# Attention outputs computed turned: values as weights, probabilities as moving data

## The chip, the cores and the metric

The kernel runs on one core of a Trainium2 chip, in float32. The metric is the device time of one execution in microseconds, the median of several runs. TensorE multiplies; VectorE (DVE), ScalarE (ACT) and GpSimd (POOL) do the elementwise work; SyncE (SP) and GpSimd issue transfers.

## The reference

A two-layer network over 18 tiles of 128 tokens: 2 tiles of a prompt (256 tokens) and 16 of a sample (2048 tokens). Each layer normalizes and modulates its input, projects it to 4096 columns, runs four token mixers of four heads of 64, multiplies each by a SiLU gate, and projects back. Two of the mixers are softmax attention, and they are all that the change touches:

```
s_loc = q @ k_near * scale + bias           # window of +-128 tokens, or a neighbourhood in the grid
s_ctx = q @ k_ctx  * scale                  # 256 further tokens; prompt tiles have only 256 own tokens
p = softmax(concat([s_loc, s_ctx]))
o = p @ concat([v_near, v_ctx])             # then o * silu(gate)
```

The window attention ("win") has a sink in its softmax and shares keys and values between heads; the neighbourhood attention ("nei") has a bias table. The two other mixers are retention ("ret") and a gated recurrence ("hg").

## The kernel before

Each engine has its own instruction stream, written out in order; they meet only at semaphores. A layer has these stages: "first" (a part of the projections), "win", "nei", "rest" (retention and the recurrence, and the output projection). The engines meet at a barrier (`gate`) after the first three; TensorE only reports there (`leave`) and goes on.

In an attention stage a unit `u` is one pair of heads of one tile: `tau, p = divmod(u, 2)`. The stage is a loop over 37 slots. In slot `s`, TensorE computes the scores of unit `s` and transposes and weighs unit `s-1`; between these steps it fills in eight projection matmuls (`fill`, L1161), which is one piece of 128x512 per slot. TensorE never needs a unit sooner than a slot after its scores.

- `scores(u)` (L1266, L1270) writes PSUM banks 2 to 5, the two heads of the pair in the two row halves of the array.
- VectorE's `maxima(u)` (L2119 to L2144) adds the mask or bias and finds row maxima; ScalarE's `exps(u)` (L1727) makes the probabilities `a.e`, queries on partitions.
- `turn(u, f)` (L1279) transposes the probabilities, 128 keys at a time and up to four such chunks at once, into bank 6 (`TURN_BANK`). ScalarE (fills 0 and 2) or VectorE (fill 1) copies them to `a.pT` (L1712, L2152).
- `weigh(u, f)` (L1297) multiplies with the values, into bank 7 (`OUT_BANK`). The stationary weights are a half (64 queries) of a chunk of `a.pT`, the moving data are 64 columns of values, and the two halves of the queries go to the two column halves of the array.
- VectorE's `finish(tau)` (L2176) multiplies bank 7 by the gates, which hold one over the softmax's sum (L2168), at the head of slot `2*tau+3`; GpSimd stores the tile.
- `prep(slot)` (L1226) transposes queries and keys for coming units, also through bank 6. In "win" this is in even slots; in "nei" from slot 5 on, queries are in even slots and keys in odd ones.

`fills_of(n)` lists the chunks of a unit with `n` chunks per head. A prompt tile has 2 chunks per head, a sample tile 4 or 5 in "win" and 5 or 6 in "nei", so a unit is one, two or three fills of four or two chunks. `count_attention` plans beforehand who used bank 6 last (`use.before`) and which semaphore count tells that it was emptied.

ScalarE's loop in a slot is: copy the finished projection piece, `take_prep`, `take_turned(.., 0)`, `exps`, `take_turned(.., 2)`, and for pieces of group 6 `bounds_ln` (L1668), two logarithms that wait for VectorE; in "nei" this is in slots 33 and 34. VectorE's is: `finish`, `maxima`, `take_turned`, `weigh_gates`, `gates` (the SiLU of a piece, L2017 to L2022, with a reciprocal), `bounds`, and in "win" `rotate_for`.

Of the kernel before, what the change touches and what calls it, by code (L numbers as in the profile page):

```python
# [13 lines left out]
P = 128  # L14
# [6 lines left out]
HD = 64  # L21
# [198 lines left out]
def fills_of(n):  # L220

    chunks = [(hp, c) for hp in range(2) for c in range(n)]
    return [chunks[i:i + 4] for i in range(0, len(chunks), 4)]
# [48 lines left out]
def count_attention(names, near_of, preps_of, k_inc, q_inc):  # L272
    made, previous = {}, None
    n = Counts()
    for l in range(DEPTH):
        for name in names:
# [7 lines left out]
            def use(key, by_act):  # L284
                nonlocal previous
                u = p.use[key] = Use()
                u.before, previous = previous, u
                n.turned += 1
                u.turned, u.by_act = n.turned, by_act
                if by_act:  # L290
                    n.by_act += 1
                    u.taken = n.by_act
                else:
                    n.by_dve += 1
                    u.taken = n.by_dve

            for slot in range(-2, 2 * NT + 1):
                for item in p.preps.get(slot, ()):
# [11 lines left out]
                if p.preps.get(slot):  # L310
                    use(("prep", slot), True)
                if slot >= 1:
# [35 lines left out]
def build(nc, ins, outs):  # L348
# [49 lines left out]
    def attention(s, name, cq, ck, cv, cg, cache_k, cache_v, col, keys):  # L398
# [5 lines left out]
        a.gate_t = sb(s, f"{name}_gate_t", [P, 2, GW])  # L404
        a.out_t = sb(s, f"{name}_out_t", [P, 2, GW])
        a.qT = sb(s, f"{name}_qT", [P, 2, 2, P])
        a.e = sb(s, f"{name}_e", [P, 2, 2, 6 * P])
# [122 lines left out]
    act_step, dve_step = sem("act_step"), sem("dve_step")  # L530
    yr_step = sem("yr_step")
    rstd_ready = sem("rstd_ready")
# [18 lines left out]
    def gate(eng, l, stage):  # L551
# [11 lines left out]
    scored, nm_ready, e_ready, weighed, out_ready = (  # L563
        sem(x) for x in ("scored", "nm_ready", "e_ready", "weighed", "attention_ready"))
    mask_in, sink_ready = sem("mask_in"), sem("sink_ready")
    bias_in = [sem(f"bias_in{k}") for k in range(3)]
    bias_clear, band_in, neg_ready, tables_out = (sem(x) for x in ("bias_clear", "band_in", "neg_ready", "tables_out"))

    for a, name in ((ret, "ret"), (hg, "hg")):
        (a.bk_ready, a.bkv_done, a.bs_ready, a.kf_ready, a.kv_done, a.sf_ready, a.var_ready, a.r_ready, a.out_ready, a.n_step) = (  # L570
            sem(f"{name}_{x}") for x in ("bk_ready", "bkv_done", "bs_ready", "kf_ready", "kv_done", "sf_ready", "var_ready",
                                         "r_ready", "out_ready", "n_step"))
        a.s_in, a.s_saved, a.clear, a.tab_in, a.p_done, a.p_ready, a.o_done = (
# [7 lines left out]
        sem(f"hg_{x}") for x in ("gated", "qk_ready", "qx_ready", "tc_ready", "ones_ready", "ks_ready"))  # L581
    dec_dve, dec_act = (sem(x) for x in ("dec_dve", "dec_act"))
    bank_turned, bank_taken = sem("bank_turned"), sem("bank_taken")
    y_taken, y_scaled = sem("y_taken"), sem("y_scaled")


    def taken(eng, use):

        if use is not None:
            eng.wait_ge(taken_act if use.by_act else taken_dve, use.taken)  # L590

# [351 lines left out]
    def _(pool):  # L943
# [11 lines left out]
        pool.wait_ge(tables_out, 16)  # L955
        pool.wait_ge(dec_dve, DEC_DVE)
        pool.dma_start(decays, dec_new[:, :, :]).then_inc(tables_out, 16)
# [171 lines left out]
    def _(pe):  # L1129
        pe.wait_ge(consts_in, 48)  # L1130
        pe.wait_ge(setup, SETUP_COND)
        for l in range(DEPTH):
# [65 lines left out]
            for a in (win, nei):  # L1198
# [83 lines left out]
                def weigh(u, f):  # L1282
                    tau, p = divmod(u, 2)
                    n = plan.near(tau) + CT
                    if f == 0 and p == 0:
                        need(pe, out_ready, plan.tile + tau)
                        if a is nei:
# [5 lines left out]
                    for i, (hp, c) in enumerate(fills_of(n)[f]):  # L1293
                        h = head_of(a, p, hp)
                        for half in range(2):
                            at = i * P + half * HD
                            last = nc.tensor.matmul(ps[half * HD:(half + 1) * HD, OUT_BANK, h * HD:(h + 1) * HD], a.pT[:, f, at:at + HD],  # L1297
                                                    values_of(tau, h)[c], start=(c == 0), stop=(c == n - 1))
                    last.then_inc(weighed, 1)

                fill(LEAD * KC)
# [288 lines left out]
    def _(act):  # L1590
# [5 lines left out]
        act.wait_ge(vectors_in, 16 * (2 * DEPTH + 8))  # L1596
        decay = Own(act, dec_act)
        for d in range(DEPTH):
            at = DEC_DVE // DEPTH * d
            act.wait_ge(dec_dve, at + 2)  # L1600
# [3 lines left out]
            act.wait_ge(dec_dve, at + 6)  # L1604
            decay.mark(nc.scalar.activation(dec_new[:, d, D_PAIR:D_PAIR + 4].rearrange("p (a g) -> p a g", g=2), lgp[:, :, :],
# [8 lines left out]
            for h in range(HEADS):  # L1614
                act.wait_ge(dec_dve, at + 7 + 3 * h)
# [4 lines left out]
        own = Own(act, act_step)  # L1620
        for l in range(DEPTH):
# [59 lines left out]
            for a in (win, nei):  # L1681
# [32 lines left out]
                def exps(u):  # L1714
# [22 lines left out]
                for slot in range(2 * NT + 1):  # L1737
                    piece = pieces[slot - 1 + LEAD] if slot > 0 else None
                    if piece:
                        take_piece(*piece)  # L1740
# [8 lines left out]
                    if piece and piece[0] == 6:  # L1749
                        bounds_ln(*piece)  # L1750
                gate(act, l, a.stage)
            pieces = PROJ_ORDER["rest"]

            def norm_stats(a, t):
                u, st = l * NT + t, a.st[:, t % 2]
                steps = Steps(act, a.n_step, u)
                act.wait_ge(a.var_ready, u + 1)
                steps.mark(nc.scalar.activation(st[:, 2], st[:, 1], ACT.Ln, bias=eps[:, 0:1], scale=1.0 / HD))
                steps.wait()
                nc.scalar.activation(st[:, 3], st[:, 2], ACT.Exp, scale=-0.5).then_inc(a.r_ready, 1)  # L1760
# [79 lines left out]
            def scale_y(t):  # L1840
                u, b = l * NT + t, t % 2
                steps = Steps(act, yr_step, u * 2)
                act.wait_ge(y_taken, 2 * u + 2)
                need(act, yr_ready, u)
                rstd(y_t[:, b], b, steps, yr_ready, y_sq[:, :], y_stat)

# [61 lines left out]
    def _(dve):  # L1908
# [33 lines left out]
        dve.wait_ge(vectors_in, 16 * (2 * DEPTH + 8))  # L1942
        decay = Own(dve, dec_dve)
        for d in range(DEPTH):
            at = DEC_ACT // DEPTH * d
            if d > 0:
                dve.wait_ge(dec_act, at)
# [3 lines left out]
            dve.wait_ge(dec_act, at + 2)  # L1951
            decay.mark(nc.vector.tensor_scalar(lg_t[:, 2], lg[:, d], 0.0, None, ALU.min))
# [6 lines left out]
            dve.wait_ge(dec_act, at + 9)  # L1959
            keys = dec_new[:, d, D_KEY:D_KEY + 2 * HEADS]  # L1960
            decay.mark(nc.vector.tensor_scalar(keys, keys, HD ** -0.5, None, ALU.mult))
            for h in range(HEADS):
                dve.wait_ge(dec_act, at + 9 + 2 * (h + 1))
                decay.mark(nc.vector.tensor_tensor(dtmp[:, 0], dtmp[:, 0], dtab[:, 2], ALU.mult))
# [4 lines left out]
        assert decay.n == DEC_DVE, decay.n  # L1969
        own = Own(dve, dve_step)  # L1970
        for l in range(DEPTH):
# [103 lines left out]
            for a in (win, nei):  # L2075
# [446 lines left out]
```

## Time and profile before

| | |
|---|---|
| runs | 4083.63 us median of 3 (4082.23 to 4086.58) |
| the profiled execution | 4087.09 us, span 4085.3 us, mean granted TensorE clock 0.968 |
| TensorE busy | 3830.6 us (94%), 24448 matmul records |
| VectorE, ScalarE, GpSimd busy | 2406.2 us (59%), 1204.5 us (29%), 572.2 us (14%) |
| chain that ended last | TensorE 85%, VectorE 7%, ScalarE 2%, DMA 2% |

A busy share is an average over stages. Matmuls are pipelined, so a record's duration is longer than the distance between two starts; the timeline's start times say what a group of matmuls takes. A float32 matmul leaves two records, a transpose one.

### The profile page before, as it was taken

The page shows a single profiled execution, that of the slowest core. Times are in us where ns is not written, and L with a number is a line of the kernel's source. Part 1 is how long each engine was busy: PE and PEld are TensorE (multiplying, and loading weights), DVE is VectorE, ACT ScalarE, POOL GpSimd, SP SyncE. Part 2 cuts the span into 40 slices and gives each one's busy share as a digit, 9 for nine tenths or more (in the row PEclk, how much of TensorE's full clock was granted, in tenths as well). Part 3 has the DMA queues.
Part 4 walks back from the last instruction along what each step waited for, and adds up shares of the span by engine and source line. Part 5 has one row for each costly group of instructions (what it writes and reads, how often), then busy time and mean ns, then how long its engine had stood idle before and what let it go on. Part 6 is the DMA issues. An engine that isn't in the chain of part 4 may idle for free.

```text
span 4085.3 us, 63551 instructions
## 1 busy us (share of the span) xinstructions
PE 3830.6 (94%) x24448; PEld 2070.8 (51%) x24448; DVE 2406.2 (59%) x4838; ACT 1204.5 (29%) x3401; POOL 572.2 (14%) x870
## 2 busy tenths in 40 slices
PE   5999999999998998899999999999999989979997
PEld 2544555545554455455544445554555445555554
DVE  3223345323666887899932333552256688879996
ACT  2411232223331122344443022222333212224443
POOL 2000000100000254110000000001000005521000
PEclk7999999999998998899999999999999999979999
DMA  7432121132222334223333021113222233333222
GB/s 233 126 132 96 56 68 53 61 105 67 87 79 92 114 102 153 93 97 113 116 109 97 39 95 50 68 43 120 74 77 73 85 104 118 107 127 122 96 94 69
DMA packets 247772, 388.91 MB, mean 95 GB/s; under 512 B 42736, under 2 KB 163440, under 8 KB 247344
## 3 DMA queue, kind: packets, MB, share of 16 engines
q1 hardware_dynamic: 207504, 262.55, 20.7%
q0 software_dynamic: 39968, 122.30, 8.2%
q8 instruction: 195, 3.19, 0.3%
q14 instruction: 105, 0.86, 0.1%
HBM read 264.42 MB, written 122.25 MB: 95 GB/s over the span
## 4 chain that ended last, share of the span: by engine, by line
PE 85%; DVE 7%; ACT 2%; DMA 2%; SPq 2%; issue 2%; POOLq 1%; POOL 0%; ACTq 0%; DVEq 0%
PE ps L1161 47%; PE ps L1511 12%; PE ps L1297 5%; PE ps L1279 4%; PE ps L1266 3%; PE ps L1464 2%; PE ps L1270 2%; PE ps L1429 1%; DVE ret_qd L2255 1%; PE ps L1408 1%; ACT mT L1810 1%; DVE e_t L2019 1%; PE ps L1339 1%; PE ps L1226 1%; PE ps L1489 1%
## 5 line engine op out<-in xcount | busy, mean ns | idle before, releaser
L1161 PE MATMUL ps<-w_sb,hT 128*128 128x512 f32 x4608 | 2204.2, 612 | 3.7 <-ACT hT L1642 2.4
L1161 PEld LDWEIGHTS ps<-w_sb,hT 128*128 128x128 f32 x4608 | 815.8, 192 | 768.8 <-issue 729.9
L1511 PE MATMUL ps<-wo_sb,mT 128*128 128x512 f32 x1152 | 533.1, 607 | 50.8 <-ACT mT L1810 50.8
L979 POOL DMA_DIRECT2D projected<-row_t x252 | 138.2, 548 | 2483.1 <-DVE row_t L2022 1086.1
L2019 DVE RECIPROCAL e_t<-e_t 128x256 f32<-128x256 f32 (+1 forms) x180 | 430.8, 2393 | 6.2
L1511 PEld LDWEIGHTS ps<-wo_sb,mT 128*128 128x128 f32 x1152 | 209.3, 191 | 282.7 <-issue 212.2
L2017 DVE TENSOR_SCALAR e_t<-e_t 128x256 f32<-128x256 f32 (+1 forms) x180 | 71.1, 395 | 238.9 <-ACT row_t L1660 207.8
L1654 ACT ACTIVATE row_t<-ps 128x512 f32<-128x512 f32 x108 | 64.5, 597 | 394.3 <-PE ps L1161 351.8
L2119 DVE TENSOR_REDUCE nei_st<-ps 128x2 f32<-128x512 f32 x72 | 49.8, 691 | 208.7 <-PE ps L1270 208.7
L2152 DVE COPY win_pT<-ps 128x512 f32<-128x512 f32 x64 | 44.3, 692 | 213.4 <-PE ps L1279 213.4
L2152 DVE COPY nei_pT<-ps 128x512 f32<-128x512 f32 x64 | 44.3, 692 | 207.8 <-PE ps L1279 207.8
L2119 DVE TENSOR_REDUCE win_st<-ps 128x2 f32<-128x512 f32 x72 | 49.6, 690 | 193.8 <-PE ps L1270 193.8
L2316 DVE TENSOR_TENSOR hg_q<-hg_d,hg_xT 128x256 f32<-128x256 f32 x252 | 153.0, 607 | 12.5 <-issue 6.1
L1712 ACT ACTIVATE win_pT<-ps 128x512 f32<-128x512 f32 (+1 forms) x128 | 64.5, 504 | 313.3 <-PE ps L1279 313.3
L1279 PEld LDWEIGHTS ps<-ident,nei_e 128*128 128x128 f32 x736 | 92.8, 141 | 105.6 <-issue 103.0
L1712 ACT ACTIVATE nei_pT<-ps 128x512 f32<-128x512 f32 (+1 forms) x136 | 74.4, 547 | 242.9 <-PE ps L1279 242.9
L1659 ACT ACTIVATE e_t<-ps 128x256 f32<-128x256 f32 x108 | 41.3, 382 | 350.7 <-PE ps L1161 349.9
L2351 DVE TENSOR_REDUCE hg_tc<-hg_w 128x64 f32<-128x448 f32 x144 | 132.9, 923 | 4.9
L1279 PEld LDWEIGHTS ps<-ident,win_e 128*128 128x128 f32 x656 | 83.6, 141 | 102.2 <-issue 100.3
L1999 DVE TENSOR_SCALAR xt<-xt,stat 128x1024 f32<-128x1024 f32 x36 | 27.1, 755 | 174.2 <-ACT stat L1630 174.2
L1297 PEld LDWEIGHTS ps<-win_v,win_pT 128*64 128x64 f32 x2624 | 92.0, 137 | 73.8 <-issue 73.2
L1829 ACT ACTIVATE hg_p<-hg_tc 64x64 f32<-64x64 f32 x288 | 73.2, 254 | 177.5 <-DVE hg_tc L2351 174.9
(243 smaller groups left out, 5355.1 us busy)
## 6 DMA issues: line engine op xcount, KB each, us to landing
projected<-row_t POOLq DMA_DIRECT2D x288, 256.0 KB, 2.8
w_sb<-in_w_in SPq DMA_DIRECT2D x14, 2048.0 KB, 9.3
wa<-in_w_ada SPq DMA_DIRECT2D x16, 1536.0 KB, 8.0
hg_raw<-projected SPq DMA_DIRECT2D x72, 256.0 KB, 4.8
out_streams<-y_t POOLq DMA_DIRECT2D x36, 512.0 KB, 4.2
hg_braw<-projected SPq DMA_DIRECT2D x108, 128.0 KB, 2.4
hg_raw<-projected SPq DMA_DIRECT2D x36, 384.0 KB, 5.2
mx_t<-mixed SPq DMA_DIRECT2D x36, 384.0 KB, 4.6
```

Source lines behind the costliest of these rows:

```text
L979: pool.dma_start(rows[tok(t), g * GRP:(g + 1) * GRP], row_t[:, p.slot]).then_inc(row_stored[p.slot], 16)
L1161: mm = nc.tensor.matmul(ps[:, p.bank, :], hT[:, k, t * P:(t + 1) * P], w_sb[:, g % 2, k, :], start=(k == 0), stop=(k == KC - 1))
L1266: nc.tensor.matmul(s[:, 0:n], q, k, start=True, stop=True)
L1279: last = nc.tensor.transpose(ps[:, TURN_BANK, i * P:(i + 1) * P], a.e[:, u % 2, hp, c * P:(c + 1) * P], ident[:, :])
L1297: last = nc.tensor.matmul(ps[half * HD:(half + 1) * HD, OUT_BANK, h * HD:(h + 1) * HD], a.pT[:, f, at:at + HD], values_of(tau, h)[c], star ...
L1511: mm = nc.tensor.matmul(ps[:, 6 + g, :], mT[:, t % 2, k, :], wo_sb[:, k, g * GRP:(g + 1) * GRP], start=(k == 0), stop=(k == KC - 1))
L1712: nc.scalar.activation(a.pT[:, f, 0:n], ps[:, TURN_BANK, 0:n], ACT.Copy).then_inc(taken_act, 1)
L2019: own.mark(nc.vector.reciprocal(e, e))
L2119: own.mark(nc.vector.reduce_max(st[:, MX, pair_at], both[:, :, n:n + CTX], AX_X))
L2152: nc.vector.tensor_copy(a.pT[:, 1, 0:n], ps[:, TURN_BANK, 0:n]).then_inc(taken_dve, 1)
L2316: own.mark(nc.vector.tensor_tensor(halves(q), halves(d, size + s, TO_END * size), halves(x), ALU.mult))
L2351: nc.vector.tensor_reduce(hg.tc[:, h % 2, :], hg.w[:, :, :].rearrange("p s n -> p n s"), AX_X, ALU.add).then_inc(hg.tc_ready, 1)
```

## The change

`weigh` takes the values as weights (128 keys by 64) and a whole chunk of `a.pT` (128 keys by 128 queries) as moving data. One matmul replaces two. Each head's output then stands turned (64 features on partitions, 128 queries in columns), the two heads of the pair in the two column halves of the array; `fills_of` is reordered so that the heads alternate. Outputs of a tile fill `OUT_BANK` as before. ScalarE copies them to `a.oT` (`take_out`) at the head of its slot `2*tau+3`, before it copies the projection piece. TensorE transposes the two 128x128 blocks into bank 6 (`turn_out`), after the scores of that slot, or at the end of the loop for the last tile. `finish` then waits for `turn_out` and reads bank 6 instead of bank 7; for "win" with the heads' order rearranged. The next user of bank 6 waits for `finish`. `weigh` waits for ScalarE's copy (`out_taken`) where it waited for `finish`. Besides, several own-order semaphores are merged into one per engine.

```diff
-    chunks = [(hp, c) for hp in range(2) for c in range(n)]
+    chunks = [(hp, c) for c in range(n) for hp in range(2)]
...
-            for slot in range(-2, 2 * NT + 1):
+            for slot in range(-2, 2 * NT + 2):
+                if slot >= 3 and slot % 2 == 1:
+                    use(("o", (slot - 3) // 2), None)
...
+        a.oT = sb(s, f"{name}_oT", [P, 2, P])
...
-            eng.wait_ge(taken_act if use.by_act else taken_dve, use.taken)
+            eng.wait_ge(out_ready if use.by_act is None else taken_act if use.by_act else taken_dve, use.taken)
...
                     if f == 0 and p == 0:
-                        need(pe, out_ready, plan.tile + tau)
+                        need(pe, out_taken, plan.tile + tau)
...
-                        for half in range(2):
-                            at = i * P + half * HD
-                            last = nc.tensor.matmul(ps[half * HD:(half + 1) * HD, OUT_BANK, h * HD:(h + 1) * HD], a.pT[:, f, at:at + HD],
-                                                    values_of(tau, h)[c], start=(c == 0), stop=(c == n - 1))
+                        last = nc.tensor.matmul(ps[hp * HD:(hp + 1) * HD, OUT_BANK, p * P:(p + 1) * P], values_of(tau, h)[c],
+                                                a.pT[:, f, i * P:(i + 1) * P], start=(c == 0), stop=(c == n - 1))
                     last.then_inc(weighed, 1)
+
+                def turn_out(tau):
+
+                    use = plan.use["o", tau]
+                    pe.wait_ge(out_taken, plan.tile + tau + 1)
+                    taken(pe, use.before)
+                    for p in range(2):
+                        last = nc.tensor.transpose(ps[:, TURN_BANK, p * P:(p + 1) * P], a.oT[:, p, :], ident[:, :])
+                    last.then_inc(turned_in, 1)
...
                         scores(slot)
+                        if slot >= 3 and slot % 2 == 1:
+                            turn_out((slot - 3) // 2)
                         fill(1)
...
+                turn_out(NT - 1)
                 leave(pe)
...
+                def take_out(tau):
+                    act.wait_ge(weighed, plan.weighed[2 * tau + 1, len(fills_of(plan.near(tau) + CT)) - 1])
+                    if tau > 0:
+                        act.wait_ge(turned_in, plan.use["o", tau - 1].turned)
+                    nc.scalar.activation(a.oT[:, :, :], ps[:, OUT_BANK, 0:GW].rearrange("p (k n) -> p k n", n=P), ACT.Copy
+                                         ).then_inc(out_taken, 1)
...
+                    if slot >= 3 and slot % 2 == 1:
+                        take_out((slot - 3) // 2)
                     if piece:
                         take_piece(*piece)
...
-                    dve.wait_ge(weighed, plan.weighed[2 * tau + 1, len(fills_of(plan.near(tau) + CT)) - 1])
+                    dve.wait_ge(turned_in, plan.use["o", tau].turned)
...
-                    nc.vector.tensor_tensor(a.out_t[:, b], ps[:, OUT_BANK, 0:GW], a.gate_t[:, b], ALU.mult).then_inc(out_ready, 1)
+                    out, o, g = a.out_t[:, b], ps[:, TURN_BANK, 0:GW], a.gate_t[:, b]
+                    if a is win:
+                        out, g = (x.rearrange("t (k p n) -> t p k n", k=2, n=HD) for x in (out, g))
+                        o = o.rearrange("t (p k n) -> t p k n", k=2, n=HD)
+                    nc.vector.tensor_tensor(out, o, g, ALU.mult).then_inc(out_ready, 1)
```

## Rows read from the trace of the kernel before

**Rows 1.** The page's part 4: the chain that ended last, by line.
```profile
PE ps L1161 47%; PE ps L1511 12%; PE ps L1297 5%; PE ps L1279 4%; PE ps L1266 3%; PE ps L1464 2%; PE ps L1270 2%; PE ps L1429 1%; DVE ret_qd L2255 1%; PE ps L1408 1%; ACT mT L1810 1%; DVE e_t L2019 1%; PE ps L1339 1%; PE ps L1226 1%; PE ps L1489 1%
```

**Rows 2.** Windows in "win" and "nei", layer 0: width, busy (instructions) by engine, clock, DMA.
```profile
400.00:790.00 390.00, 390.00 (x2569) 214.24 (x2568) 180.90 (x482) 113.58 (x299) 31.03 (x55) 1.00 0.17 54
850.00:1239.00 389.00, 389.00 (x2661) 213.78 (x2660) 201.13 (x344) 123.58 (x270) 28.20 (x50) 1.00 0.24 75
```

**Rows 3.** Groups by line and form, TensorE: the transposes of probabilities.
```profile
L1279 PE MATMUL ps<-ident,nei_e 128*128 128x128 f32 x736 | 113.8, 274 | 1.7 <-ACT nei_pT L1712 1.4 <-DVE nei_pT L2152 0.3
L1279 PE MATMUL ps<-ident,win_e 128*128 128x128 f32 x656 | 103.1, 273 | 1.5 <-ACT win_pT L1712 1.5
```

**Rows 4.** Timeline of TensorE in "nei" into an odd slot: start, us, line, records.
```profile
1004.09 0.69 PE L1297 MATMUL ps<-nei_v,nei_pT 128*64 128x64 f32 x16
1004.71 1.13 PE L1161 MATMUL ps<-w_sb,hT 128*128 128x512 f32 x2
...
1009.35 1.13 PE L1266 MATMUL ps<-nei_kT,nei_qT 64*128 64x512 f32 x4
1010.31 0.60 PE L1270 MATMUL ps<-nei_kT_past,nei_qT 64*128 64x256 f32 x4
1010.84 1.12 PE L1161 MATMUL ps<-w_sb,hT 128*128 128x512 f32 x2
1011.80 0.60 PE L1226 MATMUL ps<-ident,nei_k_raw 128*128 128x128 f32 x4
1012.24 1.88 PE L1161 MATMUL ps<-w_sb,hT 128*128 128x512 f32 x4
```

**Rows 5.** Timeline of TensorE in "win": a fill of two chunks, and the next group.
```profile
639.17 0.45 PE L1297 MATMUL ps<-win_v,win_pT 128*64 128x64 f32 x8
639.55 0.92 PE L1266 MATMUL ps<-win_kT,win_qT 64*128 64x384 f32 x4
```

**Rows 6.** Timelines of TensorE in other stages: groups with 128 moving columns.
```profile
304.27 1.92 PE L1139 MATMUL ps<-wa,cond 128*2 128x128 f32 x48
306.13 2.41 PE L1161 MATMUL ps<-w_sb,hT 128*128 128x512 f32 x5
...
1411.87 0.71 PE L1387 MATMUL ps<-ret_xT 64*128 64x128 f32 x8
1412.51 1.98 PE L1161 MATMUL ps<-w_sb,hT 128*128 128x512 f32 x4
```

**Rows 7.** Timeline of VectorE in the same odd slot.
```profile
1010.95 0.69 DVE L2119 TENSOR_REDUCE nei_st<-ps 128x2 f32<-128x512 f32 x1 [0.74 <-PE ps L1270]
...
1013.20 0.17 DVE L2138 TENSOR_SCALAR nei_st<-nei_st 128x2 f32<-128x2 f32 x1
```

**Rows 8.** Timeline of ScalarE in the same odd slot.
```profile
1015.09 0.90 ACT L1727 ACTIVATE nei_e<-ps,nei_st 128x768 f32<-128x768 f32 x1
```

**Rows 9.** Timelines of TensorE and ScalarE at the head of "nei" slot 35.
```profile
1229.24 1.98 PE L1161 MATMUL ps<-w_sb,hT 128*128 128x512 f32 x4
...
1230.67 0.36 ACT L1659 ACTIVATE e_t<-ps 128x256 f32<-128x256 f32 x1
```

**Rows 10.** Timelines of TensorE and VectorE at the ends of "win" and "nei".
```profile
793.01 0.69 PE L1297 MATMUL ps<-win_v,win_pT 128*64 128x64 f32 x16 [0.17 <-DVE win_pT L2152]
793.81 0.69 PE L1161 MATMUL ps<-w_sb,hT 128*128 128x512 f32 x1
...
1243.11 0.45 PE L1297 MATMUL ps<-nei_v_past,nei_pT 128*64 128x64 f32 x8
...
1245.05 0.42 DVE L2176 TENSOR_TENSOR nei_out_t<-ps,nei_gate_t 128x256 f32<-128x256 f32 x1
...
1262.94 0.38 PE L1339 MATMUL ps<-ret_braw,ret_bkd 128*64 128x64 f32 x2 [5.13 <-DVE ret_bkd L2222]
```

**Rows 11.** A wait of TensorE in "rest", and a window (clock third from last) after it.
```profile
1464.46 0.66 PE L1408 MATMUL ps<-ret_raw,ret_p 128*128 128x64 f32 x4 [1.19 <-DVE ret_p L2263]
...
1466.10:1469.60 3.50, 3.50 (x8) 1.78 (x6) 2.53 (x1) 0.00 (x0) 0.00 (x0) 0.51 0.10 37
```

More of the change, by code:

```diff
@@ L289, in use @@
                 u.turned, u.by_act = n.turned, by_act
-                if by_act:
+                if by_act is None:
+                    u.taken = p.tile + key[1] + 1
+                elif by_act:
                     n.by_act += 1
@@ L311, in count_attention @@
                     use(("prep", slot), True)
-                if slot >= 1:
+                if 1 <= slot <= 2 * NT:
                     tau = (slot - 1) // 2
@@ L530, in build @@
     act_step, dve_step = sem("act_step"), sem("dve_step")
-    yr_step = sem("yr_step")
     rstd_ready = sem("rstd_ready")
@@ L564, in build @@
         sem(x) for x in ("scored", "nm_ready", "e_ready", "weighed", "attention_ready"))
+    out_taken = sem("out_taken")
     mask_in, sink_ready = sem("mask_in"), sem("sink_ready")
@@ L569, in build @@
     for a, name in ((ret, "ret"), (hg, "hg")):
-        (a.bk_ready, a.bkv_done, a.bs_ready, a.kf_ready, a.kv_done, a.sf_ready, a.var_ready, a.r_ready, a.out_ready, a.n_step) = (
+        (a.bk_ready, a.bkv_done, a.bs_ready, a.kf_ready, a.kv_done, a.sf_ready, a.var_ready, a.r_ready, a.out_ready) = (
             sem(f"{name}_{x}") for x in ("bk_ready", "bkv_done", "bs_ready", "kf_ready", "kv_done", "sf_ready", "var_ready",
-                                         "r_ready", "out_ready", "n_step"))
+                                         "r_ready", "out_ready"))
         a.s_in, a.s_saved, a.clear, a.tab_in, a.p_done, a.p_ready, a.o_done = (
@@ L581, in build @@
         sem(f"hg_{x}") for x in ("gated", "qk_ready", "qx_ready", "tc_ready", "ones_ready", "ks_ready"))
-    dec_dve, dec_act = (sem(x) for x in ("dec_dve", "dec_act"))
     bank_turned, bank_taken = sem("bank_turned"), sem("bank_taken")
-    y_taken, y_scaled = sem("y_taken"), sem("y_scaled")
+    y_taken = sem("y_taken")
     def taken(eng, use):
         if use is not None:
-            eng.wait_ge(taken_act if use.by_act else taken_dve, use.taken)
+            eng.wait_ge(out_ready if use.by_act is None else taken_act if use.by_act else taken_dve, use.taken)
     def piece_out(eng, p):
@@ L955, in _ @@
         pool.wait_ge(tables_out, 16)
-        pool.wait_ge(dec_dve, DEC_DVE)
+        pool.wait_ge(dve_step, DEC_DVE)
         pool.dma_start(decays, dec_new[:, :, :]).then_inc(tables_out, 16)
@@ L1596, in _ @@
         act.wait_ge(vectors_in, 16 * (2 * DEPTH + 8))
-        decay = Own(act, dec_act)
+        own = decay = Own(act, act_step)
         for d in range(DEPTH):
             at = DEC_DVE // DEPTH * d
-            act.wait_ge(dec_dve, at + 2)
+            act.wait_ge(dve_step, at + 2)
             decay.mark(nc.scalar.activation(lg_t[:, 1], lg_t[:, 1], ACT.Exp))
@@ L1603, in _ @@
             decay.mark(nc.scalar.activation(lg_t[:, 1], lg_t[:, 1], ACT.Ln, bias=ones[:, 0:1]))
-            act.wait_ge(dec_dve, at + 6)
+            act.wait_ge(dve_step, at + 6)
             decay.mark(nc.scalar.activation(dec_new[:, d, D_PAIR:D_PAIR + 4].rearrange("p (a g) -> p a g", g=2), lgp[:, :, :],
@@ L1614, in _ @@
             for h in range(HEADS):
-                act.wait_ge(dec_dve, at + 7 + 3 * h)
+                act.wait_ge(dve_step, at + 7 + 3 * h)
                 for way in range(2):
@@ L1619, in _ @@
         assert decay.n == DEC_ACT
-        own = Own(act, act_step)
         for l in range(DEPTH):
@@ L1750, in _ @@
                         bounds_ln(*piece)
+                take_out(NT - 1)
                 gate(act, l, a.stage)
@@ L1755, in norm_stats @@
                 u, st = l * NT + t, a.st[:, t % 2]
-                steps = Steps(act, a.n_step, u)
                 act.wait_ge(a.var_ready, u + 1)
-                steps.mark(nc.scalar.activation(st[:, 2], st[:, 1], ACT.Ln, bias=eps[:, 0:1], scale=1.0 / HD))
-                steps.wait()
+                own.mark(nc.scalar.activation(st[:, 2], st[:, 1], ACT.Ln, bias=eps[:, 0:1], scale=1.0 / HD))
+                own.wait()
                 nc.scalar.activation(st[:, 3], st[:, 2], ACT.Exp, scale=-0.5).then_inc(a.r_ready, 1)
@@ L1841, in scale_y @@
                 u, b = l * NT + t, t % 2
-                steps = Steps(act, yr_step, u * 2)
                 act.wait_ge(y_taken, 2 * u + 2)
                 need(act, yr_ready, u)
-                rstd(y_t[:, b], b, steps, yr_ready, y_sq[:, :], y_stat)
+                rstd(y_t[:, b], b, own, yr_ready, y_sq[:, :], y_stat)
             for m in range(BACK_SLOTS):
@@ L1942, in _ @@
         dve.wait_ge(vectors_in, 16 * (2 * DEPTH + 8))
-        decay = Own(dve, dec_dve)
+        own = decay = Own(dve, dve_step)
         for d in range(DEPTH):
@@ L1946, in _ @@
             if d > 0:
-                dve.wait_ge(dec_act, at)
+                dve.wait_ge(act_step, at)
             decay.mark(nc.vector.tensor_scalar(lg_t[:, 0], lg[:, d], -1.0, None, ALU.mult))
@@ L1950, in _ @@
             decay.mark(nc.vector.tensor_tensor(lg_t[:, 1], lg_t[:, 0], lg[:, d], ALU.min))
-            dve.wait_ge(dec_act, at + 2)
+            dve.wait_ge(act_step, at + 2)
             decay.mark(nc.vector.tensor_scalar(lg_t[:, 2], lg[:, d], 0.0, None, ALU.min))
@@ L1958, in _ @@
                 decay.mark(nc.vector.tensor_copy(lgp[part, :, :], lg[part, d].rearrange("p (a g h) -> p a g h", a=2, g=2)[:, :, :, hp]))
-            dve.wait_ge(dec_act, at + 9)
+            dve.wait_ge(act_step, at + 9)
             keys = dec_new[:, d, D_KEY:D_KEY + 2 * HEADS]
@@ L1962, in _ @@
             for h in range(HEADS):
-                dve.wait_ge(dec_act, at + 9 + 2 * (h + 1))
+                dve.wait_ge(act_step, at + 9 + 2 * (h + 1))
                 decay.mark(nc.vector.tensor_tensor(dtmp[:, 0], dtmp[:, 0], dtab[:, 2], ALU.mult))
@@ L1969, in _ @@
         assert decay.n == DEC_DVE, decay.n
-        own = Own(dve, dve_step)
         for l in range(DEPTH):
```

## The prediction

> **What bounds the kernel now.** I read the chain of waits first, to see which engine carries the time. It names TensorE lines in order of share: the projections (L1161) take 47% of the span, the weighing matmuls that the change rewrites (L1297) 5% [rows 1]. Next I asked for busy time in the two attention stages: in each, TensorE is busy for the whole stretch (390.00 of 390.00 us, 389.00 of 389.00) at granted clock 1.00, while VectorE is busy for about half and ScalarE for less than a third [rows 2]. So here a TensorE instruction added or removed counts in full, and work on the others counts only if TensorE comes to wait for it. The rest is reading TensorE's timeline by start times, since pitches and not durations add up.
>
> **The change on TensorE.** The unit is a chunk of 128 keys for one head; each is transposed once before weighing, and a transpose leaves one record, so there are 736 + 656 = 1392 [rows 3]. Every other matmul leaves two. Before, a chunk is two matmuls (four records) of 64 moving columns, its halves in the two column halves of the array. After, it is one matmul (two records) of 128 moving columns, and the two heads of the pair take the two halves, which the new order in `fills_of` alternates. By the code there are 304 fills of four chunks and 88 of two (304 x 4 + 88 x 2 = 1392).
>
> *Weighing.* From a fill's start to the next group's start: 1004.09 to 1004.71 is 0.62 us for 16 records [rows 4], 639.17 to 639.55 is 0.38 for 8 [rows 5]. The difference, 0.24, is four steps of two parallel records, 0.06 each; what is left, 0.62 - 8 x 0.06, is about 0.15 for entering and draining the split array. For 128 moving columns in column strips the row is L1139: three strips at once, 48 records from 304.27 to 306.13, 16 steps in 1.86, so 0.116 a step with the ends and about 0.11 without [rows 6]. The strips do work in parallel although each has its own moving data. After, a fill of four chunks is then 4 x 0.11 + 0.15 = 0.59, and of two 0.37. The streaming is the same; only some overhead goes. With the rounding of the rows I take -0.025 for each of the 304 (-7.6) and -0.01 for each of the 88 (-0.9): **-8.5 us**. The bound from above is L1387: 8 records of 128 columns, from 1411.87 to 1412.51, 0.64 [rows 6], which would make it +0.02 x 304 + 0.03 x 88 = +8.7. I don't take it because its weights are 128 columns wide, and on entering a mode the weight load lies open: 64 columns are loaded here. The bound from below is a step shorter than 0.11, which is the rival below.
>
> The Trainium skill (TensorEngine Tiling, Performance Considerations, Instruction Overhead) says each matmul carries about 60 cycles of overhead and one with a single column takes as long as one with 60. If that were on top of the streaming, the 1392 steps removed would give, by an estimate from that page, 1392 x 25 ns = -35 us at 2.4 GHz, and the whole change would end near 4070. The rows above leave about 6 ns a step for it, so I keep them.
>
> *Turning back.* New: two 128x128 transposes per tile, 72 tiles. Four transposes go from 1011.80 to 1012.24 [rows 4], so two cost 0.22. They stand between the scores and the first projection matmul, where the array goes back to full mode anyway, so no further switch comes. 66 tiles pay: 66 x 0.22 = **+14.5 us**. Of the other six, two are slot 3 of the neighbourhood stage, just before a wait for keys, and four are at the stage ends, below.
>
> *Waits in an ordinary odd slot.* The new chain is last weighing, ScalarE copy, two transposes, VectorE's gate product, and only then the next user of bank 6. The scores take 1009.35 to 1010.84, 1.49 us [rows 4]; the copy needs some 0.04 + 0.38 + 0.04, ready a second early (0.38 is the kind of 128x256 read at 1230.67, 0.36, in [rows 9]; 0.04 is from the end of the scores, 1010.91, to VectorE's start at 1010.95 [rows 4, 7]). So the transposes don't wait. They end about 0.22 + 0.27 after 1010.84; the product (0.42, as at 1245.05 in [rows 10]) then ends near 1011.8, where the first bank-6 user, the key transposes, stood at 1011.80 and moves to 1012.02 [rows 4]. Its weights want loading some 0.1 earlier, so this is close, and I put 0 on it: nearly 0.1 is left. In window slots three projection matmuls stand before the next user. VectorE's row maximum starts 0.77 later than at 1010.95 and its last step ends near 1014.1 in place of 1013.37 [rows 7]; ScalarE's exponentials start at 1015.09 anyway [rows 8]. The next work of VectorE and of ScalarE waits for TensorE later in the slot, so nothing further is late.
>
> *Neighbourhood slot 35.* The copy of tile 16 stands behind `bounds_ln`, which waits for VectorE. In ScalarE's order the first work behind it starts at 1230.67 [rows 9]. So the copy ends near 1231.05 and the transposes, due at 1229.24, start near 1231.1: TensorE stands 1.9 us, once a layer: **+3.8 us**. Nothing takes it back, as the rest of that stage is paced by TensorE.
>
> *Stage ends.* The last tile has no cover. In the window stage the weighing ends at 793.70 and the projections go on at 793.81 [rows 10]. Now between them: 0.04 + 0.38 + 0.05 for the copy, 0.22 for the first transpose with its weight load, 0.27 for the second, and the same 0.11, 1.07 in all, +0.96: **+1.9 us** for two. At the end of the neighbourhood stage about as much is added, but TensorE then waits 5.13 us for VectorE [rows 10], and VectorE starts its last gate product only at 1245.05, when the weighing has ended at 1243.56 [rows 10]: the turned outputs would be there by 1244.6, so VectorE isn't made later; so +0. Slot 3 goes into the keys' wait likewise.
>
> *Clock.* After a wait of 1.19 us at 1464.46 the granted clock of the next 3.5 us is 0.51, the lower level of 1.2 GHz [rows 11]. One such stretch costs half of it, 1.7 us. Four waits of about that size are new; that one in four is followed by it is my choice: **+1.7**.
>
> Renamed semaphores and the reordered `own` counters order the same instructions in the same way: 0.
>
> Sum: -8.5 + 14.5 + 3.8 + 1.9 + 1.7 = **+13.4 us**. The profiled execution took 4087.1 around its span of 4085.3, so it would read 4100.5; it is 3.5 above the median of the runs, and on the median, 4083.6, I forecast **4097.0**.
>
> **Rivals.** (a) *A wait at bank 6.* If the product ends after the key transposes' due time, each of the 28 neighbourhood slots with keys pays some 0.3: +8, 4105. For it: the 0.1 of room. Against: VectorE is free in time in these slots. (b) *The strips serialize* at 128 columns: +0.43 in each full fill, 304 x 0.43 + 88 x 0.21 = +149, 4246. L1139 speaks against it. (c) *Not slower.* The step of 128 columns is cheaper than 0.11, since each record carries a fixed part. All else costs 21.9, so it decides at 0.07 a fill, a step of 0.09; at 0.085 it gives about -44 + 22, 4062. Against: 0.11 in L1139 and in the transposes alike. (d) *No change to measure*: the entry to the split array gets cheaper by some 0.02 and slot 35 and the clock cost little: -14 + 14.5 + 3 + 2, 4089. A measurement of this kernel tells about 0.2% (8.2 us) from nothing.
>
> **How the numbers follow.** My case 0.65, (a) 0.07, (b) 0.04, (c) 0.07, (d) 0.17. Slower: the first three, 0.76. Same 0.17, faster 0.07. Range: down to (d), up to (a) plus part of the L1387 bound: 4088 to 4110; it leaves out (b), (c) and the far part of that bound.
>
> **What would show it.** Right: L1297 at half its records; fills of 0.59 and 0.37; a pair of transposes in 0.22 right after the scores; TensorE still without waits in ordinary slots; one wait of 1.9 us on ScalarE at slot 35 in each layer. Wrong: a 128-column step other than 0.11, a wait for the gate product before the key transposes, or late maxima that reach TensorE.

## The result, and the profile after

The changed kernel takes 4096.27 us, median of 9 runs (4091.24 to 4098.92), against 4085.20 for the kernel before, median of 9 (4080.36 to 4087.06). The ratio is 1.0028, 95% interval 1.0018 to 1.0039: slower by 11 us, between 7 and 16. The forecast was 13.4 slower, and the measured time lies in its range.

The profiled execution took 4091.24 us around a span of 4089.4. That is the fastest run of this kernel, and the one of before was above all of its own, so the spans (4.1 apart) understate the change. I read the traces for terms, and take totals from the medians.

The chain by line, as in [rows 1], and the two windows of [rows 2] for the changed kernel (L1165 are the projections, L1299 the weighing):

```profile
PE ps L1165 46%; PE ps L1525 12%; PE ps L1299 5%; PE ps L1283 4%; PE ps L1270 3%; PE ps L1478 2%; PE ps L1274 2%; PE ps L1443 1%; DVE ret_qd L2279 1%; DVE e_t L2039 1%; PE ps L1422 1%; ACT mT L1832 1%; PE ps L1353 1%; PE ps L1503 1%; PE ps L1230 1%
```
```profile
400.00:790.00 390.00, 389.26 (x1967) 204.92 (x1968) 180.45 (x482) 118.98 (x317) 31.50 (x56) 1.00 0.17 54
850.00:1239.00 389.00, 387.14 (x1985) 203.39 (x1984) 200.50 (x344) 127.96 (x286) 27.64 (x49) 1.00 0.23 74
```

TensorE still carries both stages: all that it lacks in these windows are one wait of 0.74 that the first window now just takes in, and one of 1.86 in the second.

TensorE's timeline into an odd slot of the neighbourhood stage, against [rows 4], and a fill of two chunks in the window stage, against [rows 5]:

```profile
1004.57 0.66 PE L1299 MATMUL ps<-nei_pT,nei_v 128*64 128x128 f32 x8
1005.15 1.98 PE L1165 MATMUL ps<-w_sb,hT 128*128 128x512 f32 x4
...
1008.62 0.60 PE L1274 MATMUL ps<-nei_kT_past,nei_qT 64*128 64x256 f32 x4
1009.14 0.44 PE L1309 MATMUL ps<-ident,nei_oT 128*128 128x128 f32 x2
1009.42 1.02 PE L1165 MATMUL ps<-w_sb,hT 128*128 128x512 f32 x2
1010.28 0.60 PE L1230 MATMUL ps<-ident,nei_k_raw 128*128 128x128 f32 x4
```
```profile
637.12 0.44 PE L1299 MATMUL ps<-win_pT,win_v 128*64 128x128 f32 x4
637.49 0.92 PE L1270 MATMUL ps<-win_kT,win_qT 64*128 64x384 f32 x4
```

A full fill takes 1005.15 - 1004.57 = 0.58 (0.588 in the mean of the trace's start times, where before had 0.615), one of two chunks 0.37 (0.369 against 0.382). The two transposes (L1309) take 1009.14 to 1009.42, 0.27 to the next start. But the two projection records behind them take 0.86, 1009.42 to 1010.28, where they took 0.96 in [rows 4]: the entry to the full array has moved into the transposes. So the pair costs 0.17 net. The key transposes (L1230) follow without a wait. In the window stage the pair costs the same: 0.27 again, and six projection records behind it take 2.58 where they took 2.68.

VectorE and ScalarE in the same odd slot, against [rows 7] and [rows 8], and TensorE's weight load (PEld) for the key transposes:

```profile
1009.62 0.42 DVE L2200 TENSOR_TENSOR nei_out_t<-ps,nei_gate_t 128x256 f32<-128x256 f32 x1 [1.35 <-PE ps L1309]
...
1012.20 0.17 DVE L2158 TENSOR_SCALAR nei_st<-nei_st 128x2 f32<-128x2 f32 x1
```
```profile
1007.77 0.38 ACT L1748 ACTIVATE nei_oT<-ps 128x256 f32<-128x256 f32 x1 [2.50 <-PE ps L1299]
...
1013.57 0.89 ACT L1740 ACTIVATE nei_e<-ps,nei_st 128x768 f32<-128x768 f32 x1
```
```profile
1010.10 0.54 PEld L1230 LDWEIGHTS ps<-ident,nei_k_raw 128*128 128x128 f32 x4 [0.48 <-DVE nei_out_t L2200]
```

The copy is done at 1008.15, a second before the transposes. The gate product ends at 1010.04, 0.24 before the key transposes start. But their weight load did wait for it: it starts at 1010.10, 0.18 before the first of them, where it started 0.43 ahead in the kernel before. So the product is just in time. The maxima end at 1012.37, still 1.2 before the exponentials begin. All the new work of these two engines is covered here.

Not covered are slot 35 and the stage ends. The first three rows below are TensorE and ScalarE in slot 35, against [rows 9]; the others are TensorE at the stage ends, against [rows 10]:

```profile
1229.67 0.44 PE L1309 MATMUL ps<-ident,nei_oT 128*128 128x128 f32 x2 [1.85 <-ACT nei_oT L1748]
...
1228.74 0.61 ACT L1681 ACTIVATE f_t<-f_t 128x512 f32<-128x512 f32 x1
1229.26 0.36 ACT L1748 ACTIVATE nei_oT<-ps 128x256 f32<-128x256 f32 x1
...
792.44 0.44 PE L1309 MATMUL ps<-ident,win_oT 128*128 128x128 f32 x2 [0.48 <-ACT win_oT L1748]
792.98 1.55 PE L1165 MATMUL ps<-w_sb,hT 128*128 128x512 f32 x3
...
1244.57 0.44 PE L1309 MATMUL ps<-ident,nei_oT 128*128 128x128 f32 x2 [0.49 <-ACT nei_oT L1748]
1245.26 13.97 PE L1165 MATMUL ps<-w_sb,hT 128*128 128x512 f32 x32 [0.26 <-issue]
1262.18 0.70 PE L1353 MATMUL ps<-ret_braw,ret_bkd 128*64 128x64 f32 x8 [2.94 <-DVE ret_bkd L2246]
```

In slot 35 the copy stands behind the logarithms (L1681) and TensorE waits 1.85. TensorE's waits over the whole program (total, times, longest) have two new lines, and one that moves by itself:

```profile
PE ps L1353 <- DVE ret_bkd L2246: 40.2, 12, 6.9
...
PE ps L1230 <- DMA nei_k_raw<-projected: 7.6, 4, 3.0
...
PE ps L1309 <- ACT nei_oT L1748: 4.7, 4, 1.9
...
PE ps L1309 <- ACT win_oT L1748: 1.0, 2, 0.5
```

Added up from the trace: 304 fills x -0.027 and 88 x -0.013 give -9.4; 66 pairs in the slots x 0.174, +11.5 (the two of slot 3 stand before the wait for keys); slot 35, 2 x 1.86, +3.7; window ends, 2 x 0.9, +1.8. That is +8, at the low end of the measured interval.

### The profile page after: what moved, and what is told of

The parts are those of the page before. It is cut to its first block, busy times and chain, and to the rows that moved or that the text cites. A ratio compares the mean times of both kernels' runs of the same rounds, so it can differ in the third digit from the quotient of the medians.

```text
span 4089.4 us, 58483 instructions
## 1 busy us (share of the span) xinstructions
PE 3827.7 (94%) x21808; PEld 2030.7 (50%) x21808; DVE 2403.0 (59%) x4838; ACT 1224.0 (30%) x3473; POOL 572.8 (14%) x870
## 4 chain that ended last, share of the span: by engine, by line
PE 84%; DVE 7%; ACT 3%; SPq 2%; DMA 2%; issue 2%; POOLq 1%; POOL 0%; DVEq 0%; ACTq 0%
PE ps L1165 46%; PE ps L1525 12%; PE ps L1299 5%; PE ps L1283 4%; PE ps L1270 3%; PE ps L1478 2%; PE ps L1274 2%; PE ps L1443 1%; DVE ret_qd L2279 1%; DVE e_t L2039 1%; PE ps L1422 1%; ACT mT L1832 1%; PE ps L1353 1%; PE ps L1503 1%; PE ps L1230 1%
## 5 line engine op out<-in xcount | busy, mean ns | idle before, releaser
L1165 PE MATMUL ps<-w_sb,hT 128*128 128x512 f32 x4608 | 2192.2, 609 | 3.7 <-ACT hT L1655 2.4
L1165 PEld LDWEIGHTS ps<-w_sb,hT 128*128 128x128 f32 x4608 | 814.7, 191 | 782.1 <-issue 766.9
L1098 POOL DMA_DIRECT2D out_streams<-y_t x36 | 21.0, 584 | 719.5 <-DVE y_t L2403 719.5
```

Of the source, the lines that this page charges most:

```text
L1165: mm = nc.tensor.matmul(ps[:, p.bank, :], hT[:, k, t * P:(t + 1) * P], w_sb[:, g % 2, k, :], start=(k == 0), stop=(k == KC - 1))
```

## The experiments

Each is compared with runs of the kernel before on the same chip. The interval of a difference is 4 to 6 us either way. The ratio is not exactly that of the medians; a difference worked out from it can be 2 us off theirs.

**Weighing alone.** The new matmuls and order of chunks, without copy and turning back. The outputs are read as they stand, so features and queries change places in the attention's output.

```diff
-                    dve.wait_ge(turned_in, plan.use["o", tau].turned)
+                    dve.wait_ge(weighed, plan.weighed[2 * tau + 1, len(fills_of(plan.near(tau) + CT)) - 1])
...
-                    out, o, g = a.out_t[:, b], ps[:, TURN_BANK, 0:GW], a.gate_t[:, b]
+                    out, o, g = a.out_t[:, b], ps[:, OUT_BANK, 0:GW], a.gate_t[:, b]
```
The calls of `take_out` and `turn_out` and their place in the plan are gone too, and `weigh` waits for the gate product again.

> The changed kernel with its new weighing alone: nothing is copied and turned back, and the gate product reads the turned outputs straight from bank 7, so the attention outputs are multiplied with the gates of other places. My theory: a fill of four chunks takes 0.59 us where it took 0.615, one of two 0.37 where it took 0.38, so the kernel is about 9 us faster than before (ratio 0.998), near 4076, and TensorE waits nowhere that it did not wait before. Rival, that the weighing itself is what got slower (its two strips in part serialized at 128 columns): 10 us or more above before.

Measured: 4074.56 against 4082.88, ratio 0.9979 (0.9971 to 0.9988), by the ratio 8.6 us faster. The fills take 0.588 and 0.369 as in the changed kernel. The new weighing is a gain by itself, of the size forecast, and the rival falls. This kernel also carries the merged semaphores, and it ends about 1 us from the -9.4 of its fills, so nothing is seen of their cost.

**Turning back alone.** The changed kernel with the old matmuls and the old order of chunks; outputs that were not turned are turned.

```diff
-                        last = nc.tensor.matmul(ps[hp * HD:(hp + 1) * HD, OUT_BANK, p * P:(p + 1) * P], values_of(tau, h)[c],
-                                                a.pT[:, f, i * P:(i + 1) * P], start=(c == 0), stop=(c == n - 1))
+                        for half in range(2):
+                            at = i * P + half * HD
+                            last = nc.tensor.matmul(ps[half * HD:(half + 1) * HD, OUT_BANK, h * HD:(h + 1) * HD], a.pT[:, f, at:at + HD],
+                                                    values_of(tau, h)[c], start=(c == 0), stop=(c == n - 1))
```

> The changed kernel with the old weighing: two matmuls of 64 columns a chunk, and then the copy and the turning back of outputs that were not turned, so that queries and features change places in the attention output. My theory: 68 pairs of transposes at 0.17 to 0.22 us each in the slots, two waits of 1.9 us at slot 35, some 1 us at each end of a window stage: 17 to 21 us above before, 4102 to 4106. Rival, that the transposes are hidden and only the new waits cost: 6 us above before, 4091.

Measured: 4105.97, ratio 1.0053 (1.0040 to 1.0065), by the ratio 21.6 us slower. The transposes are not hidden. With the run above, -8.6 + 21.6 = +13.0, and the whole change comes to +11.4 and, below, +12.2 by its ratios: the two parts add up within the intervals, which would not show a third of a few us.

**All of one head first.** One line of the changed kernel, the old order of chunks:

```diff
-    chunks = [(hp, c) for c in range(n) for hp in range(2)]
+    chunks = [(hp, c) for hp in range(2) for c in range(n)]
```

> The changed kernel with the old order of chunks, all of one head before the other, with the same result. My theory: the gain of weighing rests on neighbouring matmuls going to different column halves. A fill of four chunks of one head then streams 8 records one after the other, 8 x 0.11 + 0.15 = 1.03 us in place of 0.59; mixed fills are in between; some 0.35 us on 304 fills and 0.22 on 88, 100 to 130 us above the changed kernel. Rival, that the array overlaps whatever stands in its queue: no difference to the changed kernel.

Measured: 4198.26, ratio 1.0278 (1.0263 to 1.0294), 103 us above the changed kernel on the same chip. TensorE's timeline of a fill of one head only, and of the next fill, two chunks of one head and then two of the other:

```profile
1027.88 1.09 PE L1299 MATMUL ps<-nei_pT,nei_v 128*64 128x128 f32 x8
1028.89 1.12 PE L1165 MATMUL ps<-w_sb,hT 128*128 128x512 f32 x2
...
1030.39 0.32 PE L1299 MATMUL ps<-nei_pT,nei_v_past 128*64 128x128 f32 x1
1030.40 0.32 PE L1299 MATMUL ps<-nei_pT,nei_v 128*64 128x128 f32 x1
...
1030.98 1.55 PE L1165 MATMUL ps<-w_sb,hT 128*128 128x512 f32 x3
```

The fill of one head takes 1.01 us in place of 0.58. But the second fill takes 0.59, and its records start in pairs, 0.013 apart, one of each head (`nei_v_past` holds the first head's last two chunks, `nei_v` the other head's first two), although the kernel issues both matmuls of one head first. So neighbours in the queue need not go to different halves: here the matmul two places further on ran beside. Over the trace, full fills of one head take 1.02, those of one and three chunks 0.81, the 48 of two and two 0.59, and the small fills, all of one head, 0.58 in place of 0.37. What counts is that a fill holds both heads in equal shares. In most fills of this order it does not, and so the new form is a clear loss with it. The rival is wrong for the kernel's time, but has a part of the truth.

**The changed kernel again**, for a second trace.

> The changed kernel as it is, for a second trace of it. My theory: 4096 us again; both slot-35 waits at 1.86 us, both window ends at 0.48 us of wait. The wait for keys at the third slot of the neighbourhood stage (2.7 and 3.0 us in the first trace, 2.8 and 0.8 in that of before) and the stretches of lower clock change from run to run: if they belong to the change, they come out alike here.

Measured: 4095.37, ratio 1.0030 (1.0019 to 1.0042). The waits on the copies are the same to 0.01 us (4.7 in four, 1.0 in two). The keys' waits came to 5.5 us here and 7.6 in the first trace, 5.1 in that of before. They differ between traces of one kernel, so their change is not the kernel's.

**Slot 35 covered.** The turning back of that one tile stands two projection matmuls later.

```diff
+                        late = a is nei and slot == 2 * NT - 1
-                        if slot >= 3 and slot % 2 == 1:
+                        if slot >= 3 and slot % 2 == 1 and not late:
                             turn_out((slot - 3) // 2)
                         fill(1)
+                        if late:
+                            fill(1)
+                            turn_out((slot - 3) // 2)
...
-                        fill(2)
+                        fill(2 - late)
```

> The changed kernel, but in slot 35 of the neighbourhood stage the turning back stands behind the first two projection matmuls instead of ahead of them, so that ScalarE's late copy of that tile (it stands behind two logarithms) is covered. My theory: the wait of 1.86 us there goes or shrinks to 0.1, once a layer, and nothing else moves: 3.7 us off, near 4092. Rival, that the stage was waiting for VectorE there in any case: the time comes back as a wait before the next transposes of probabilities, and the kernel stays at 4096.

Measured: 4091.21, ratio 1.0016 (1.0007 to 1.0024), 4 to 6 us less than the changed kernel in its two sets of runs. The intervals of the ratios just overlap, so here the trace decides. TensorE's timeline in slot 35 with the weight load (PEld) of the transposes, and its waits on the copies:

```profile
1230.44 1.98 PE L1165 MATMUL ps<-w_sb,hT 128*128 128x512 f32 x4
1232.37 0.44 PE L1309 MATMUL ps<-ident,nei_oT 128*128 128x128 f32 x2
1232.64 1.02 PE L1165 MATMUL ps<-w_sb,hT 128*128 128x512 f32 x2
1233.50 0.60 PE L1283 MATMUL ps<-ident,nei_e 128*128 128x128 f32 x4
...
1232.36 0.20 PEld L1309 LDWEIGHTS ps<-ident,nei_oT 128*128 128x128 f32 x2 [0.77 <-ACT nei_oT L1752]
```
```profile
PE ps L1309 <- ACT nei_oT L1752: 1.0, 2, 0.5
PE ps L1309 <- ACT win_oT L1752: 1.0, 2, 0.5
```

The two waits of 1.86 are gone, and no other came in their place. A small rest is left: the weight load still waited for the copy, which ends at 1232.31, and the four projection records ahead take 1.93, which is 0.11 more than the 1.82 that is left of 2.68 for six behind other scores, less 0.86 for two. The pair, its load late, takes 0.27, and away from the scores nothing behind it gets shorter.

**Each turning back issued twice.**

```diff
-                    for p in range(2):
+                    for p in (0, 1, 0, 1):
```

> The changed kernel with the two transposes of each turning back issued twice, with the same result. My theory: a further pair costs its pitch, 2 x 0.109 us, in 72 places, of which 68 to 70 count: 15 us more, 4111; a group of four takes 0.49 us to the next start where one of two takes 0.27. Since the next group loses 0.10 us of its own in exchange, the first pair costs 0.17 net, less than the second. Rival, that transposes hide in the drain of the scores: under 5 us more.

Measured: 4107.42, ratio 1.0054 (1.0042 to 1.0067), 11 us more than the changed kernel's first median, where 15 were expected and the intervals allow both. TensorE's timeline:

```profile
639.67 0.66 PE L1309 MATMUL ps<-ident,win_oT 128*128 128x128 f32 x4
640.16 1.02 PE L1165 MATMUL ps<-w_sb,hT 128*128 128x512 f32 x2
```

0.49 for four where two took 0.27: a further pair costs 0.22, the first 0.17. The added pair is not hidden anywhere, so the rival falls.

**Weighings grouped, on the kernel before.** The switches into and out of the split array cost more than the steps that the change shortens, so this takes switches away instead.

```diff
                     if n > 1:
                         turn(slot - 1, 1)
-                    if n > 0:
-                        weigh(slot - 1, 0)
                     fill(more)
                     if n > 2:
                         turn(slot - 1, 2)
-                    if n > 1:
-                        weigh(slot - 1, 1)
                     fill(2 * more)
-                    if n > 2:
-                        weigh(slot - 1, 2)
+                    for f in range(n):
+                        weigh(slot - 1, f)
```

> The kernel before with the fills of a unit weighed one after the other at the end of the slot instead of apart among the projections, with the same result. My theory: a weighing group costs about 0.35 us beyond its steps, since TensorE drains and reloads where it enters and leaves the split array (0.09 before it, 0.15 in it, 0.10 behind it). 120 units lose two such groups and 8 lose one: 248 x 0.35 = 87 us less, near 3996. Rival, that a burst of more than 16 records runs at a slower pitch or waits for the copies of probabilities: half of that gain or less.

Measured: 4014.43 against 4083.46, ratio 0.9828 (0.9814 to 0.9841): 69 us faster. The same kernel on another chip, 4017.26, ratio 0.9834 (0.9820 to 0.9849). TensorE's timeline:

```profile
646.63 1.02 PE L1161 MATMUL ps<-w_sb,hT 128*128 128x512 f32 x2
647.58 0.44 PE L1279 MATMUL ps<-ident,win_e 128*128 128x128 f32 x2
647.85 1.88 PE L1161 MATMUL ps<-w_sb,hT 128*128 128x512 f32 x4
649.66 1.39 PE L1297 MATMUL ps<-win_v,win_pT 128*64 128x64 f32 x40
650.98 0.92 PE L1266 MATMUL ps<-win_kT,win_qT 64*128 64x384 f32 x4
```

VectorE's copy of bank 6 in the same slot, and the weight load for the two transposes at 647.58:

```profile
646.83 0.69 DVE L2148 COPY win_pT<-ps 128x512 f32<-128x512 f32 x1 [3.55 <-PE ps L1279]
647.58 0.20 PEld L1279 LDWEIGHTS ps<-ident,win_e 128*128 128x128 f32 x2 [0.75 <-DVE win_pT L2148]
```

The 40 records take 1.32, where 16 + 16 + 8 took 0.62 + 0.62 + 0.38. The pitch holds through a long burst, so that rival falls. The missing 18 us are to be seen above: two projection records take 0.95, not 0.86, and the third group's two transposes 0.27, not 0.22, together 0.14 in each of 120 units, 17 us. The last two lines say why: the copy ends at 647.52, and the weight load, which waited for it, comes only then.

**The same grouping on the changed kernel.**

> The changed kernel with its weighings grouped in the same way. My theory: it gains about as much as the kernel before does by the same edit, 80 to 90 us, so it ends 8 to 15 us behind that one, near 4008. With fewer, longer records the weighing itself should gain at most some 0.03 us a fill beside the old one, as in its ungrouped form. Rival, that the new form suffers from the grouping less than the old one because it has half the instructions: then it ends level with it or ahead.

Measured: 4031.08, ratio 0.9874 (0.9859 to 0.9889), 17 us behind the grouped kernel before. The order of the two forms stays, and here too the rival falls. The distance is somewhat over what I expected. TensorE's timeline in slot 35, and the window behind it (clock third from last):

```profile
1195.69 0.44 PE L1309 MATMUL ps<-ident,nei_oT 128*128 128x128 f32 x2 [2.40 <-ACT nei_oT L1744]
1195.96 4.44 PE L1165 MATMUL ps<-w_sb,hT 128*128 128x512 f32 x6
...
1196.20:1199.60 3.40, 3.40 (x5) 1.35 (x4) 2.38 (x7) 0.00 (x0) 1.10 (x2) 0.50 0.40 155
```

The wait is 2.40, up from 1.86, and behind it the granted clock falls to 0.50 (1.2 GHz) for 3.4 us: six projection records take 4.27 in place of 2.58. Layer 1 shows the same. So slot 35 costs 4.1 a layer here. With the weighing (a unit of 20 records takes 1.24 where the old form takes 1.32), the pairs and the window ends that makes some 12 us; the two traces' spans are 11.3 apart. The rest of the 17 is not beyond the intervals.

**Grouped, with the projections set 2, 2, 1**, shown against the grouped kernel before.

```diff
                         turn(slot - 1, 1)
-                    fill(more)
+                    fill(2 * more)
                     if n > 2:
                         turn(slot - 1, 2)
-                    fill(2 * more)
+                    fill(more)
                     for f in range(n):
                         weigh(slot - 1, f)
```

> The kernel before with grouped weighings, and the projection matmuls between the three groups of transposes set 2, 2, 1 in place of 2, 1, 2, with the same result. My theory: in the grouped form two projection matmuls between the second and third group take 0.09 us longer than their pitch and the third group's first transpose another 0.055, since bank 6 is emptied a little late (VectorE's copy of 0.69 us). With two matmuls between, that goes: 0.14 us in each of 120 units, 17 us off, near 3998. Rival, that this time belongs to the order of weight loads and not to the bank, or that the last copy of probabilities is now late for the weighing: the same 4014, or a wait before the weighing.

Its neighbour on the same chip was the grouped kernel again:

> The kernel before with grouped weighings, as in the run of that name, beside the one with the fills set 2, 2, 1 on the same chip: 4014 us, ratio 0.983. If it comes out nearer 3996, the gain of grouping was understated there.

Measured: 3996.73, ratio 0.9788 (0.9774 to 0.9801), against 4017.26 for the other. TensorE's timeline:

```profile
644.13 1.88 PE L1161 MATMUL ps<-w_sb,hT 128*128 128x512 f32 x4
645.85 0.38 PE L1279 MATMUL ps<-ident,win_e 128*128 128x128 f32 x2
646.07 1.02 PE L1161 MATMUL ps<-w_sb,hT 128*128 128x512 f32 x2
647.02 1.39 PE L1297 MATMUL ps<-win_v,win_pT 128*64 128x64 f32 x40
648.34 0.92 PE L1266 MATMUL ps<-win_kT,win_qT 64*128 64x384 f32 x4
...
645.85 0.14 PEld L1279 LDWEIGHTS ps<-ident,win_e 128*128 128x128 f32 x1 [0.29 <-issue]
```

The pair takes 0.22 and nothing waits in the slot: the weight load (last line) no longer waits for VectorE, whose copy has ended at 645.02, 0.8 earlier. Elsewhere eight waits of projections for VectorE are new, 1.7 us in all. With the wait of the load in the grouped kernel this shows that the cause was bank 6, emptied late. This version computes the same outputs in 86 us less than the kernel before, and beats both kernels.

## Why the prediction was right, point by point

- **What bounds the stages:** right. TensorE was busy throughout, and each term that changed came from its own instructions or its waits.
- **Weighing, -8.5:** right. The trace gives -9.4 (0.588 and 0.369 for the forecast 0.59 and 0.37), weighing alone -8.6. The row to go by was L1139, several column strips at 128 moving columns. L1387 was rightly not gone by; that its wider weights are the reason is not shown, since no run changed them.
- **The skill's rule.** The 60 cycles a matmul of the Trainium skill (TensorEngine Tiling, Performance Considerations, Instruction Overhead) would have made weighing alone 35 us faster, by the estimate in the prediction, if they came on top of 64 columns. It measured 8.6. This kernel can't tell whether they are a floor, since its shortest matmul in question has 64 columns.
- **Turning back, +14.5:** mechanism right, size too large. The step said that no further switch comes, but left the switch's own cost where it was. It moves: the pair takes 0.27, and the projection behind it gets 0.10 shorter. Measured 0.174 a pair, +11.5 for 66.
- **Ordinary slots, 0:** right, and as close at bank 6 as forecast: the gate product ends 0.24 ahead of the key transposes, but only 0.06 ahead of their weight load, which had waited for it. Rival (a) did not come.
- **Slot 35, +3.8:** right, 1.85 us in each layer; covering it gave the time back.
- **Stage ends, +1.9:** right, 0.48 of wait and two transposes. That TensorE's delay at the end of the neighbourhood stage disappears in its wait for VectorE is seen in layer 0 only, where that wait shrank from 5.13 to 2.94; the loads in it vary by a microsecond or two from trace to trace.
- **Clock, +1.7:** not borne out in the changed kernel: behind the window ends and slot 35 the granted clock stayed at 1.00 through the new waits of 0.5 to 1.86 us. The mechanism itself came in its grouped version, where a wait of 2.40 in slot 35 was followed by 3.4 us at 0.50 in both layers.
- **The sum.** With the terms as measured it is +8; the medians say +11 and +12, with intervals from 7 to 17. What the other 3 us are, if they are real, stays open: the stretches at the lower clock add up to 266 us in the trace before and to 253 and 262 in the two of the changed kernel, and as each costs half its length, traces differ by more than that without the change. The forecast, 13.4, is nearer to the medians than its terms deserve: turning back was 3.0 too large and the clock 1.7, which is luck.
- **The other rivals:** (b), serial strips, happens only when a fill does not hold both heads in equal shares (+103 us). (c) was said to need a step of 0.09, but by its own figure, 0.07 a fill, not slower begins at (0.615 - 0.07 - 0.15) / 4 = 0.10. The step measured 0.109, so (c) still falls, with less distance. (d) needed a cheaper entry; what a fill takes beyond its steps is 0.15 in both kernels.

## What to carry to other kernels

Where TensorE is the bound, price a rewrite of its matmuls by start-to-start pitch. Swapping weights and moving data changed nothing in what is streamed and saved 0.007 us per chunk and head, while turning back cost 0.17 us a tile, so by an estimate from these numbers it pays only beyond some 24 chunks and heads a tile (here 8 to 24). What did cost were the switches between the full and the split array: putting the split-array matmuls together saved 69 us, and 86 with the other work respaced around them, ten times what the new form of the matmul could. When a new step is put on an engine's queue, look for the one slot where something late stands ahead of it, and for the last turn of the loop, which has no cover.

## What the runs showed of the hardware that was not expected

- Two column halves with different moving data run in parallel at 128 columns, 0.11 us a step. A fill whose four matmuls all go to one half takes 1.02 us in place of 0.59. With two to one half and then two to the other it takes 0.594: the matmul two places further down the queue starts 0.013 us behind the first, ahead of the one between them.
- The cost of entering the full array after scores depends on what enters: two projection records take 0.96 right behind scores and 0.86 behind the two transposes, while the transposes take 0.27 there and 0.22 among projections (`grouped_221`). So the pair costs 0.17 net.
- A weight load that waits for its bank delays its matmul even where the matmul's row shows no wait: 0.14 us a unit in the grouped kernel before, gone once the bank was free 0.8 us ahead.
- A split-array group costs 0.15 us beyond its steps however long it is: 8, 16, 40 and 48 records of 64 columns take 0.38, 0.615, 1.315 and 1.548 us, on one line at 0.029 a record.
